# Square sums of the query latent: sixteen ones-matmuls, or GpSimd adds and four ones-matmuls

## The reference

```
x = x + gate * rms_norm(y_lat, post_norm[0])
h = rms_norm(x, pre_norm[1]) * (1 + scale) + shift
c_q, c_kv, k_r, gate = split(h @ mla_w_in)
rms_norm(x, g) = x * rsqrt(mean(x * x) + 1e-6) * g      # mean over the 2048 channels
```

## Time and profile before

| | us |
|---|---|
| three runs | 1700.97, 1702.75, 1703.56 (median 1702.75) |
| the profiled execution | 1701.71 |
| its span, first to last instruction | 1699.9 |
| PE busy | 1666.6 (98%) |
| weight loads busy | 1483.6 (87%) |
| DVE busy | 1312.2 (77%) |
| ACT busy | 763.5 (45%) |
| GpSimd busy | 30.4 (2%) |

### The profile page before, as it was taken

The page is one execution under the profiler, slowest core; times in us unless marked ns, Lnnn a source line. Parts: engine busy times, 40 slices in busy tenths (PEclk is TensorE's granted clock), DMA queues, the critical chain, the costliest instruction groups (busy, mean ns, idle before and its releaser), DMA issues.

```text
span 1699.9 us, 26892 instructions
## 1 busy us (share of the span) xinstructions
PE 1666.6 (98%) x10702; PEld 1483.6 (87%) x10702; DVE 1312.2 (77%) x2150; ACT 763.5 (45%) x1184; POOL 30.4 (2%) x46
## 2 busy tenths in 40 slices
PE   9999999999999999999999999999989999999998
PEld 9999988888889788888888887889989899999886
DVE  7899778478657788788887779775897787888654
ACT  7533384624546653323332223233655455445443
POOL 0000000000000000000000000000000111100000
PEclk9999999999999999999999999999999999999999
DMA  8787766547686544346454556655345655344354
GB/s 291 244 284 265 238 199 198 188 130 245 229 309 236 174 153 145 124 135 212 161 188 160 187 197 196 194 183 171 125 149 174 194 181 160 121 135 137 98 173 138
DMA packets 163508, 315.28 MB, mean 185 GB/s; under 512 B 14508, under 2 KB 22840, under 8 KB 163128
## 3 DMA queue, kind: packets, MB, share of 16 engines
q1 hardware_dynamic: 152352, 288.92, 51.5%
q0 software_dynamic: 5312, 18.88, 3.8%
q10 hardware_dynamic: 5720, 5.78, 1.0%
HBM read 311.44 MB, written 2.10 MB: 184 GB/s over the span
## 4 chain that ended last, share of the span: by engine, by line
PE 69%; DVE 5%; ACT 1%; issue 1%; ACTq 0%; DVEq 0%
PE bank L650 16%; PE bank L651 16%; PE bank L652 16%; DVE w_low L376 2%; PE bank L3059 2%; PE bank L2643 1%; PE bank L3336 1%; PE bank L3338 1%; PE bank L3337 1%; PE bank L735 1%; PE bank L737 1%; PE bank L736 1%; PE bank L3048 1%; PE bank L2646 1%; PE bank L557 1%
## 5 line engine op out<-in xcount | busy, mean ns | idle before, releaser
L650 PE MATMUL bank<-operand,w_high 128*128 128x256 f32 (+2 forms) x2368 | 754.8, 319 | 13.0 <-DVE w_low L376 9.3
L651 PE MATMUL bank<-operand,w_high 128*128 128x256 f32 (+2 forms) x2368 | 744.2, 314 | 0.0
L652 PE MATMUL bank<-operand,w_low 128*128 128x256 f32 (+2 forms) x2368 | 744.1, 314 | 0.0
L366 ACT ACTIVATE w_high<-raw 128x1024 fp32r<-128x1024 f32 (+3 forms) x404 | 393.3, 1004 | 399.8 <-PE bank L652 172.5
L376 DVE TENSOR_TENSOR w_low<-raw,w_high 128x1024 fp32r<-128x1024 f32 (+3 forms) x404 | 451.8, 1157 | 96.8 <-ACT w_high L366 94.5
L650 PEld LDWEIGHTS bank<-operand,w_high 128*128 128x128 f32 x2368 | 452.3, 191 | 54.1 <-issue 15.1
L651 PEld LDWEIGHTS bank<-operand,w_high 128*128 128x128 f32 x2368 | 452.5, 191 | 28.0 <-issue 0.7
L652 PEld LDWEIGHTS bank<-operand,w_low 128*128 128x128 f32 x2368 | 452.3, 191 | 27.1
L521 DVE SCALAR_TENSOR_TENSOR ada_acc<-ada_raw,silu_c,ada_acc 128x512 f32<-128x512 f32 x464 | 318.8, 746 | 6.0 <-DMA ada_raw<-in_ada_w 3.7
L650 PE MATMUL bank<-operand_small,w_high 128*128 128x512 f32 (+1 forms) x240 | 89.3, 372 | 7.4 <-DVE big L489 3.8
L651 PE MATMUL bank<-operand_small,w_high 128*128 128x512 f32 (+1 forms) x240 | 87.3, 364 | 0.0
(11 more groups left out here) (443 smaller groups left out, 1919.3 us busy)
## 6 DMA issues: line engine op xcount, KB each, us to landing
ada_raw<-in_ada_w SPq DMA_DIRECT2D x160, 512.0 KB, 4.3
raw<-in_w_in SPq DMA_DIRECT2D x96, 512.0 KB, 5.1
raw<-in_pool_w_in SPq DMA_DIRECT2D x64, 512.0 KB, 5.2
raw<-in_mla_w_in SPq DMA_DIRECT2D x48, 512.0 KB, 4.5
raw<-in_w_out SPq DMA_DIRECT2D x32, 512.0 KB, 6.3
raw<-in_pool_w_out SPq DMA_DIRECT2D x32, 512.0 KB, 5.7
ada_raw<-in_ada_w POOLq DMA_DIRECT2D x32, 512.0 KB, 4.2
raw<-in_mla_w_out SPq DMA_DIRECT2D x32, 512.0 KB, 4.8
```

Of the source, the lines that this page charges most:

```text
L366: ins = nc.scalar.activation(view(HI[:, slot, ks, :], False), view(RAW[:, slot, ks, :], True), ACT.Copy)
L650: pe.matmul(out_, hi, x[:, 0, :], start=first, stop=False, skip_group_check=True)
L651: pe.matmul(out_, hi, x[:, 1, :], start=False, stop=False, skip_group_check=True)
L652: return pe.matmul(out_, lo, x[:, 0, :], start=False, stop=last, skip_group_check=True)
```

## The change

GpSimd waits for a quarter's square, adds tiles 2 and 3 to tiles 0 and 1 in place (one instruction of 128x512), waits for its own semaphore, and adds tile 1 to tile 0 (128x256). PE waits for that second add and sums tile 0 alone: one ones-matmul for each quarter in place of four. The four folds stand in GpSimd's list between the loads of units 161 and 162. ACT still waits for PE's sum before it writes the buffer again.

```diff
--- before.py
+++ after.py
@@ -908,6 +908,7 @@
 
         front_pe = steps("front_pe", [("rm",), ("rx",)])
         root_table = sem("root_table")
+        x_folded = sem("latent_squares_folded")
         front_act = steps("front_act_steps", [("h0", k) for k in range(4)] + [("hm", q) for q in range(1, 4)]
                           + [("sm", q) for q in range(4)] + [("rm",)] + [("hx", q) for q in range(4)] + [("sx", q) for q in range(4)] + [("rx",)])
         front_dve = steps("front_dve_steps", [("lm", 0), ("lm", 1), ("lm", 2), ("lm", 3), ("am", 1), ("am", 2), ("am", 3),
@@ -2898,6 +2899,14 @@
             dve_low(dve, uq[0], 0, 0)
             dve_evac(dve, mg3, 0)
 
+        def pool_fold_squares(pool, q):
+
+            post_act.wait(pool, "x", q)
+            x = SQX[q % 2]
+            nc.gpsimd.tensor_tensor(x[:, 0:2, :], x[:, 0:2, :], x[:, 2:4, :], ALU.add).then_inc(x_folded, 1)
+            pool.wait_ge(x_folded, 2 * q + 1)
+            nc.gpsimd.tensor_tensor(x[:, 0, :], x[:, 0, :], x[:, 1, :], ALU.add).then_inc(x_folded, 1)
+
         def pe_latents(pe):
             xs = lambda n, k: pe.wait_ge(xs_ready, norms[n]["xs0"] + k)
 
@@ -2908,11 +2917,9 @@
                 return ins
 
             def square_sums(q):
-                post_act.wait(pe, "x", q)
-                for k in range(4):
-                    ins = pe.matmul(PB[5][:, 0:T], ones[:, :], SQX[q % 2][:, k, :], start=q == 0 and k == 0,
-                                    stop=q == 3 and k == 3, skip_group_check=True)
-                post_pe.inc(ins, "x", q)
+                pe.wait_ge(x_folded, 2 * q + 2)
+                post_pe.inc(pe.matmul(PB[5][:, 0:T], ones[:, :], SQX[q % 2][:, 0, :], start=q == 0, stop=q == 3,
+                                      skip_group_check=True), "x", q)
 
             pe_po_half(pe, 2, 0, (1,))
             po_dve.wait(pe, "sx", 3)
@@ -3483,6 +3490,9 @@
             pool.dma_start(gb[0:4, 0:1], a["ml_bi"].rearrange("l h -> h l")).then_inc(gb_in, 16)
             pool.dma_start(gb[0:4, 1:2], a["ml_bf"].rearrange("l h -> h l")).then_inc(gb_in, 16)
             for u in range(160, UNITS["uq1", 0, 0][0]):
+                if u == 162:
+                    for q in range(4):
+                        pool_fold_squares(pool, q)
                 sp_unit(pool, u)
             pool_gate_rows(pool)
             for u in range(UNITS["uq1", 0, 0][0], 4 * 48):
```

## The result

The changed kernel takes 1709.93 us (median of six runs, 1709.2 to 1712.36) against 1703.86 us before (six runs): ratio 1.0041, 95% interval 1.0028 to 1.0054. It is slower by 6.1 us where the sum had 5.0. The predicted 1707.2 us stood on a base of 1702.2, halfway between the profiled execution and the median of three runs; the median of six is 1.6 us above that base, and against it 1707.2 is only 3.3 us more, about half of what was measured. The direction held; the terms behind the size did not.

The account below looks back on a forecast made before the run. PE's chunks and sums and DVE's loop run neck and neck, meeting at the reciprocal. DVE loses 6.8 us from 1224.89, so the reciprocal comes 5.0 later: 1706.7 on the profiled base, 1707.2 predicted halfway to the median's; range 1700.3 to 1710.2.

Parts of the forecast that it names:

- the sum: DVE loses 6.8 us up to the reciprocal, which starts at 1231.7 in place of 1226.69: 5.0 us later.
- What goes: Twelve of sixteen ones-matmuls, 4.6 us of PE; DVE's last weight half limits the reciprocal's gain to 1.80 us.
- The length of a fold: GpSimd's two adds for each quarter, put at 1.7 us together, bounds 1.12 and 5.10 us.
- the sign put down beforehand: In the trace, the fold's size is wrong if a pair of adds lasts under 1.2 us or over 2.5.
- What the adds do to DVE: Shared memory between GpSimd's adds and DVE's two-tile reads: DVE loses nothing, or stands still for the whole fold.
- The dear end: The bound taken for DVE beside the adds: it stands still for each whole fold, 4 x 1.7 = 6.8 us.
- Fold 3, itself waiting for a DVE half (1.2 us) ahead of each of its adds: Fourth quarter's fold starts at 1225.8, ends by 1229.9; PE's matmul and the root are through by 1231.1, just under DVE.
- does not absorb anything: DVE's idle 0.65 us per loop period hides no loss, being a wait for an ACT operand that follows DVE's pass.
- Adds at no cost: First rival: adds run beside DVE freely, gain 1.8 us, 1699.9 or 1700.9 us by base; chance 0.25.
- Half a cost: Second rival: both engines slow in part, DVE by half a fold, 1.6 us later, 1703.3 to 1704.4; chance 0.17.
- GpSimd starved: Third rival: GpSimd gets in only where DVE pauses, some 12 us slower, 1714; chance 0.06.
- The shift of the reciprocal: The reciprocal's 5.0 us delay carries to the kernel's end; the prediction fails if it is not found there.

Follow-up runs that it names:

- the copies: The changed kernel with each GpSimd add replaced by a copy of the same length on the same tiles, reading one tile, not two; one execution, 1706.7 us.
- the memsets: The changed kernel with each GpSimd add replaced by a 128x512 memset on a tile nobody else uses; ratio 0.9983.
- the adds apart: The kernel before, all sixteen ones-matmuls kept, plus GpSimd adds of the same sizes at the same points on tiles unused in the stage; ratio 1.0022.
- DVE adds: The changed kernel with the same folds made by DVE itself after each quarter's weight halves, none by GpSimd; ratio 1.0017.

## Why the prediction came out as it did

- **What goes.** 1.80 us were forecast, with DVE as the bound. Three kernels without GpSimd reads in the stage gave 1.88, 1.89 and 1.88.
- **The length of a fold.** 1.7 us were taken, and the rows give about that. By the sign put down beforehand (a pair of adds over 2.5 us) it would be wrong, as three of the four pairs last 4.76 to 6.01 us from first start to last end; but most of that is waiting, which the sign left out. The Trainium skill's "GPSIMD Engine Reference", section "Elementwise — side-by-side cycle accounting", gives 4497 ns for an add of 2048 columns, in proportion an estimated 1.12 us for the long add; the trace agrees, with 1.12 to 1.18 from the moment that it is let in.
- **What the adds do to DVE.** The dear end was right in kind: DVE stands still while GpSimd adds. The trace agrees with what the Trainium skill says in "SBUF — State Buffer", section "Who interferes with whom": a DVE instruction with two SBUF inputs collides with a GpSimd instruction that reads SBUF (the adds and the copies), and not with one that only writes (the memsets). What the prediction drew from that rule, that DVE loses each fold in full, did not come out: it lost 3.98 us, not 6.8.
- **The step that failed.** "Fold 3, itself waiting for a DVE half (1.2 us) ahead of each of its adds": I let GpSimd have its turn at the end of every DVE instruction, and so charged DVE 4 x 1.7 = 6.8 us. Measured are 1.49, 1.53, 0.96 and 0, together 3.98. The fourth fold took nothing from DVE, because four weight halves in a row left it no pause. In the third round the short add lay in DVE's own 0.64 us of idle time for ACT, of which the prediction had said that it "does not absorb anything". In the first two rounds DVE lost about 0.2 us less than a fold; why is open.
- **The term that was missing.** As the fourth fold ran after DVE's end, not beside it, the fold, PE's matmul at half clock and the root came behind DVE one after the other: 3.74 us idle, 2.15 more than before. I had PE and the root through just under DVE. DVE's last half is 3.77 us later (3.98, less 0.21 of its own gap closed), and 3.77 + 2.15 = 5.92. DVE's loss was put 2.8 us too high and the idle time 3.7 us too low. That the two errors nearly cancelled, so that a wrong sum landed 0.9 us from the measured shift, is luck.
- **The rivals.** Adds at no cost: excluded by the stretched rows and by the adds apart. Half a cost: DVE's 3.98 us are nearer to its 3.4 than to my 6.8, but not in its way, since each stretched instruction stands still for most of an add (the one of 16 columns for 1.11 us of 1.18) and the fourth fold costs DVE nothing. GpSimd starved: I gave it 0.06, and argued that "a waiting engine has many ends to slip in at". That argument was the failed step again; for the last fold the rival was right, while the first three were let in sooner than it had them, and its 12 us did not come.
- **The end.** The shift of the reciprocal was found again at the end: spans differ by 8.0 us, of which 2.07 were there before the stage.

## What to carry over

Before work goes to an engine whose reads collide with those of the bound engine, ask who waits when both want the memory, and look for the places in the busy engine's instruction list where the helper gets in: there the busy engine loses the helper's time, less what pause it had anyway, and where there is no such place the helper's whole length lands behind it. Price the helper against the bound engine doing the work itself, which was 3.6 us cheaper here. And a matmul that sums with ones may be made cheaper where it stands: rounding its operands gave the whole gain without moving anything, at the price of squares rounded to the shorter format.

## What was not expected of the hardware

- A run of back-to-back DVE weight halves shuts a GpSimd read out for its whole length: 5.21 us for 1.12 of work, over four instructions, and 5.49 over eight shorter ones. A pause of 0.1 us, or a wait of DVE for its own result, ends it. In the changed kernel, too, two adds got in between the passes L2819 and L2820, where DVE uses its own result and starts 0.03 to 0.04 us after its end. Which other places let GpSimd in stays open: in the first round the adds also got in between two operand instructions of 256 columns, and in the second ahead of the one of 16 columns, where the trace shows no pause.
- After 6.71 us without a matmul, PE's granted clock was 0.50 for the next stretch, and one ones-matmul took 1.22 us for 0.59. Against the same matmul after idle time at full clock (DVE adds) that is about 0.5 us on the path. It also fell in the first round of the changed kernel: PE waits 1.94 us for the stretched operands (0.44 before), starts at 1205.19, and from 1206.3 to 1209.6 the granted clock is 0.51. That cost nothing at the end, as PE waits for DVE again at 1219.73. The length of the idle time alone does not tell it: after 3.73 us in DVE adds the clock was 1.00.
